# Gathering the tokens of an expert: by rows sorted in memory instead of by a 0/1 matrix product

## What is computed

```python
def moe_swiglu(x, w_router, w_gate, w_up, w_down):
    logits = (x @ w_router).astype(jnp.float32)
    top_val, top_idx = lax.top_k(logits, TOP_K)
    wts = jax.nn.softmax(top_val, axis=-1)
    gates = jnp.sum(jax.nn.one_hot(top_idx, N_EXPERTS, dtype=jnp.float32) * wts[..., None], axis=-2)
    out = jnp.zeros_like(x)
    for e in range(N_EXPERTS):
        h = jax.nn.silu(x @ w_gate[e]) * (x @ w_up[e])
        out = out + gates[..., e:e + 1].astype(x.dtype) * (h @ w_down[e])
    return out
```

## Time and profile before

| | us |
|---|---|
| median of the three runs | 1912.5 |
| the three runs | 1922.28, 1911.4, 1912.5 |
| the profiled execution's own time | 1912.93 |
| its span (first to last instruction) | 1911.2 |

### The profile page before, as it was taken

The page is one execution under the profiler, slowest core; times in us unless marked ns, Lnnn a source line. Parts: engine busy times, 40 slices in busy tenths (PEclk is TensorE's granted clock), DMA queues, the critical chain, the costliest instruction groups (busy, mean ns, idle before and its releaser), DMA issues.

```text
span 1911.2 us, 23856 instructions
## 1 busy us (share of the span) xinstructions
PE 1775.3 (93%) x9639; PEld 1516.7 (79%) x9639; DVE 1448.3 (76%) x1270; ACT 1024.6 (54%) x804; POOL 34.1 (2%) x34
## 2 busy tenths in 40 slices
PE   2899889988979999896999999999999999999995
PEld 2888678968769997896888887888878888888884
DVE  5786865485865554675888889888888898888995
ACT  1434244453223332332776768767777677676772
POOL 0000002000000000000000000000000000000000
PEclk8899989999999999897999999999999999999998
DMA  9578254504734465443999999999999999999992
GB/s 339 195 297 330 102 218 169 183 1 149 201 131 166 144 241 183 170 175 112 334 341 352 364 371 349 342 349 367 361 334 337 368 366 349 352 360 373 354 371 102
DMA packets 214023, 511.32 MB, mean 268 GB/s; under 512 B 6998, under 2 KB 13294, under 8 KB 213913
## 3 DMA queue, kind: packets, MB, share of 16 engines
q1 hardware_dynamic: 209104, 502.46, 72.5%
q10 hardware_dynamic: 4632, 6.72, 1.0%
q0 software_dynamic: 176, 0.53, 0.1%
HBM read 507.77 MB, written 1.93 MB: 267 GB/s over the span
## 4 chain that ended last, share of the span: by engine, by line
PE 88%; DVE 6%; ACT 2%; issue 2%; DMA 1%; POOL 1%; ACTq 0%; POOLq 0%; DVEq 0%
PE psum L719 27%; PE psum L721 27%; PE psum L720 27%; PE psum L1045 2%; PE psum L1073 1%; PE psum L981 1%; DVE units L1474 1%; DMA ring<-in_mod_w 1%; POOL root_out L1441 1%; PE psum L1114 1%; DVE stats L1884 1%; DVE R L1548 0%; DVE x L1893 0%; DMA R<-in_positions 0%; DVE R L1881 0%
## 5 line engine op out<-in xcount | busy, mean ns | idle before, releaser
L1474 DVE TENSOR_TENSOR units<-ring,units 128x2048 fp32r<-128x2048 f32 x451 | 1012.7, 2278 | 239.7 <-ACT units L1180 166.8
L1382 ACT CAST units<-ring 128x2048 fp32r<-128x2048 f32 x332 | 629.7, 1914 | 245.1 <-PE psum L721 147.1
L719 PE MATMUL psum<-units,xr 128*128 128x512 f32 x1120 | 444.7, 397 | 8.0 <-issue 4.5
L721 PE MATMUL psum<-units,xr 128*128 128x512 f32 x1120 | 439.0, 392 | 0.0
L720 PE MATMUL psum<-units,xr 128*128 128x512 f32 x1120 | 438.6, 392 | 0.0
L1180 ACT CAST units<-ring 128x2048 fp32r<-128x2048 f32 (+1 forms) x119 | 218.4, 1879 | 218.3 <-PE psum L721 184.3
L719 PE MATMUL psum<-units,H 128*128 128x512 f32 x696 | 273.4, 393 | 2.2 <-DVE H L1474 2.2
L721 PE MATMUL psum<-units,H 128*128 128x512 f32 x696 | 271.5, 390 | 0.0
L720 PE MATMUL psum<-units,H 128*128 128x512 f32 x696 | 271.4, 390 | 0.0
L719 PE MATMUL psum<-xr,units 128*128 128x256 f32 x864 | 247.2, 286 | 12.4 <-DVE units L1474 11.4
L719 PEld LDWEIGHTS psum<-units,xr 128*128 128x128 f32 x1120 | 212.0, 189 | 52.8 <-issue 7.6
(11 more groups left out here) (243 smaller groups left out, 1092.0 us busy)
## 6 DMA issues: line engine op xcount, KB each, us to landing
ring<-in_moe_w_gate SPq DMA_DIRECT2D x56, 2048.0 KB, 9.4
ring<-in_moe_w_up SPq DMA_DIRECT2D x56, 2048.0 KB, 9.6
ring<-in_moe_w_down SPq DMA_DIRECT2D x56, 2048.0 KB, 9.5
ring<-in_mod_w SPq DMA_DIRECT2D x12, 2048.0 KB, 9.8
ring<-in_ret_w_in SPq DMA_DIRECT2D x11, 2048.0 KB, 10.2
ring<-in_fox_w_in SPq DMA_DIRECT2D x8, 2048.0 KB, 8.9
ring<-in_sc_w_in SPq DMA_DIRECT2D x6, 2048.0 KB, 7.8
ring<-in_ffn_w_gate SPq DMA_DIRECT2D x5, 2048.0 KB, 7.8
```

Source lines behind the costliest of these rows:

```text
L719: mm(dst, left[0], right[0], start=first, stop=False)
L721: return mm(dst, left[1], right[0], start=False, stop=last)
L1382: nc.scalar.copy(*expert_unit_parts(q, j, half, 0)).then_inc(unit_high, 1)
L1474: return v.tensor_tensor(dst, src, high.bitcast(F32), ALU.subtract)
```

## The change

Six things are new.

1. A table `x_rows` of 16 x 128 rows of 1024 numbers in the chip's memory, and an input `zeros` of 128 rows of zeros. During the loads of the dense FFN SP copies `zeros` 16 times into `x_rows`, four copies behind each of four `ffn_up` loads.
2. `places` on DVE, 11 small instructions behind `select(0, 0)`: for each token and each of its two experts the row number, expert times 128 plus place.
3. POOL writes the tokens by these numbers into `x_rows`: four indirect DMAs, of 128 rows of 4 KB each, behind the root `mix1_1` in its list.
4. `load_rows_of` on SP, between the loads j = 3 and j = 4 of each expert but the last: 128 rows (512 KB) of the next expert come back into one of the two tiles of `x`. It waits for the four writes, for the copies of `x` into `e_acc`, and for the gather before.
5. `gather_rows` on PE in the place of `gather` for experts 1 to 7: eight 128x128 transposes of the tile that was loaded. Expert 0 is gathered as before.
6. The wait for `e_sel`, which `gather` had, now stands ahead of its transposition in the down product.

```diff
+    x_rows = nc.dram_tensor("x_rows", (2 * NE, P, D), F32).ap()
...
+        place = sb("place", [P, 2, NT], I32)
...
                     stack(3)
+                for c in range(1, 5):
+                    if at == WEIGHTS_AT[CHUNK_AT["ffn_up", c]]:
+                        for n in range(4 * (c - 1), 4 * c):
+                            sp.dma_start(x_rows[n], t["zeros"]).then_inc(rows_cleared, 16)
+
+            def load_rows_of(e, q):
+
+                sp.wait_ge(rows_placed, 2 * NT * 16)
+                sp.wait_ge(gate_emptied, 2)
+                sp.wait_ge(up_emptied, 2)
+                sp.wait_ge(gather_filled, e)
+                sp.dma_start(x[:, q, :], x_rows[bass.ds(e, 1), :, :].rearrange("o p d -> (o p) d")).then_inc(rows_in, 16)
 
             def expert(e, q, more, number):
                 for j in range(PER_EXPERT):
+                    if j == 4 and more:
+                        load_rows_of(e + 1, 1 - q)
...
-            sweeps(sp, expert)
+            sweeps(sp, expert, lambda: load_rows_of(NE, 0))
...
+            def gather_rows(e, q):
+
+                pe.wait_ge(rows_in, 16 * e)
+                for k in range(KB):
+                    last = nc.tensor.transpose(psum[:, k // 4, (k % 4) * P:(k % 4 + 1) * P], x[:, q, k * P:(k + 1) * P], ident)
+                last.then_inc(gather_filled, 1)
...
                     if j == GATHER_AFTER and more:
-                        gather(e + 1, 1 - q)
+                        gather_rows(e + 1, 1 - q)
...
                         b = turn_bank(PAIRS - 1)
+                        pe.wait_ge(sel_ready, e + 1)
...
             def start_second():
-                gather(NE, 0)
+                pe.wait_ge(scatter_emptied, NE + 1)
+                gather_rows(NE, 0)
                 wide_product(NE, 0, 0)
...
+                if name == "mix1_1":
+                    pool.wait_ge(rows_cleared, 2 * NE * 16)
+                    pool.wait_ge(place_ready, 2)
+                    pool.wait_ge(x_ready, 4 * NT)
+                    for k in range(2):
+                        for tt in range(NT):
+                            at = bass.IndirectOffsetOnAxis(place[:, k, tt:tt + 1], 0)
+                            nc.gpsimd.indirect_dma_start(x_rows.rearrange("e p d -> (e p) d"), at, x[:, tt, :], None
+                                                         ).then_inc(rows_placed, 16)
...
+            def places():
+
+                step(v.tensor_scalar(rt[:, LG], rt[:, C], float(P), float((NE - 1) * P), ALU.is_gt, ALU.mult))
+                step(v.tensor_tensor(rt[:, LG], rt[:, LG], rt[:, C], ALU.add))
+                step(v.scalar_tensor_tensor(rt[:, LG], row8, -float(P), rt[:, LG], ALU.mult, ALU.add))
+                for k, hot in enumerate((OH1, OH2)):
+                    step(v.tensor_tensor(rt[:, LG2], rt[:, LG], rt[:, hot], ALU.mult))
+                    step(v.tensor_reduce(rt[:, 12, :, 0], rt[:, LG2], AX.X, ALU.add))
+                    step(v.tensor_scalar(rt[:, 13, :, 0], rt[:, 12, :, 0], float(NE * P - 1), None, ALU.add))
+                    v.tensor_copy(place[:, k, :], rt[:, 13, :, 0]).then_inc(place_ready, 1)
...
             select(0, 0)
+            places()
             gathered(0, 0)
...
+    given["zeros"] = np.zeros((P, D), np.float32)
```

More of the change, by code:

```diff
@@ L437, in build @@
         out_b = region(13312, D)
+        rows_cleared = sem("rows_cleared")
+        place_ready = sem("place_ready")
+        rows_placed = sem("rows_placed")
+        rows_in = sem("rows_in")
         slot_filled = [sem(f"slot_filled{s}") for s in range(RING)]
```

## The result

| | us |
|---|---|
| before, median of four runs | 1912.4 (1911.4 to 1922.3) |
| the changed kernel, median of four runs | 1897.1 (1896.9 to 1898.0) |
| ratio | 0.9909, 95% interval 0.9881 to 0.9936 |
| the profiled execution's own time, and its span | 1897.09, 1894.9 |

A forecast was written before the change was run, and what follows sets the result against it. PE was taken as the bound, each us off it counting until loads are late. 1912.9 - 18.3 (gathers) + 2.0 (row loads) + 0.5 (start) = 1897.1, said as 1897; the forecast's own range 1893 to 1903, overall 1893 to 1912.

The forecast's parts named there:

- PE's saving: Gathers of seven experts: eight transposes (0.87 us) replace the 3.49 us matrix product, 2.62 us less each, 18.3 in all.
- The loads behind it: 512 KB of rows ahead of load j = 4 in seven experts: 0.3 us lost per expert, 2 us in all.
- PE's cushion: First half of chunk j = 5 ready 1.4 us before PE wants it, against 1.36 us of delay by the row load.
- The hole at j = 4: Around load j = 4 of an expert, 1.7 us of DMA engines stand idle and take most of the row load's 1.36.
- The start: Before expert 0: the four indirect writes end at 900.9 or some 2 us later; 0.5 us lost, once.
- The zeros: Dense FFN: 16 copies of 512 KB, at most 10.8 us per four against some 14 us of slack; cost nothing.
- (a): Rival, experts: the loads become the bound, 1.5 to 2.6 us lost per expert, 1905 to 1913 us; chance 0.11.
- (b): Rival, experts: the load of the rows holds the queue, up to 27 us slower, 1939; chance 0.06 together with (e).
- (c): Rival, start of expert 0: slow writes by index delay load j = 4, up to 17 us once, 1913; chance 0.05.
- (d): Rival, gathers: transposes at 0.088 us and nothing lost, 1893.4 us or a little below; chance 0.06.
- (e): Rival, experts: memory's long-run limit binds; at 352 GB/s 126.7 us per expert, 1937; chance 0.06 together with (b).

The follow-up runs named there:

- The 32 transposes: The changed kernel with each gather by rows doing its eight transposes four times over, all DMAs of the change kept: 1914.4 us, ratio 0.9998.

## Why the prediction was right, and where it was lucky

Forecast 1897, measured 1897.1. The mechanism was right; that the number agrees to the tenth is not, for terms were a little off in both directions and their errors cancel.

- **PE's saving** was taken as 2.62 us per gather, 18.3 in all, from 0.109 us per transpose. It is 2.70 and 18.9. The next product starts sooner behind a transpose than another transpose does: 0.80 us from start to start, inside the bounds of 0.70 to 0.91. The earlier trace rows had it already: four transposes take 0.43 us up to the gather and 0.35 up to a wide product, and 0.87 less these 0.08 is 0.79. The 32 transposes confirm the term: 18.3 us for seven times 24 records.
- **The loads behind it** were given 2.0 us. They cost nothing (the run without them). This price is the step that failed. The room was nearly right: 387 GB/s, read from 5 us stretches, stands beside 389 to 394 over whole experts, and 5.4 us to spare beside 6 to 7. With that room in the same paragraph, I still charged 0.3 us per expert, since I took the long gather for what refills PE's cushion. I would say now that the cushion is refilled in every chunk, wherever the queue runs ahead of PE; that is argued, not shown. In the changed kernel the first half of the same chunk j = 5 is ready at 1044.51 + 2.25 = 1046.8 and wanted at 1055.07 - 5.5 = 1049.6: 2.8 us, where the kernel before had 1.4:

```profile
1044.51 4.49 DVE L1512 TENSOR_TENSOR units<-ring,units 128x2048 fp32r<-128x2048 f32 x2
...
1055.07 0.60 PE L1100 MATMUL psum<-const,R 128*128 128x128 f32 x4
```

- **The hole at j = 4** was real but not needed: ahead of j = 6 the load is as free.
- **The start**, 0.5 us, is 0. The writes were forecast to be over between 900.9 and some 2 us later; SP goes on at 902.15, in a trace that runs 0.7 us behind. An indirect write costs POOL 0.97 us by the median, as the plain DMA of the earlier trace rows had let expect, and load j = 4 is issued at 902.75, before the 905.4 from which it would be noticed. Expert 0's j = 4 to 7 show no idle time. The writes land 3.7 us after their issue (the median in each of the eight later traces; the first one lists no landing), between the 4.4 of the earlier trace rows and the 3.2 that the Trainium skill's formula (DMA: Bandwidth & Descriptors, Anatomy of one DMA) gave; neither value would have moved the sum.
- **The zeros** at nothing: right, with room for twice as many.
- **What I had not in the sum** are the 3.1 us of jumps, clock and the rest. They are as large as the 2.5 us that I had added for stalls that didn't come and the 0.6 by which I had undervalued the saving, together. A forecast from the mechanism alone, taken off the same execution of the kernel before, would have said 1894. That execution, 1912.9, was itself on the low side: the later lots of that kernel have medians of 1914.7 and 1914.1, while the changed kernel again took 1897.3. Counted from 1914.7, the saving of 18.9 and the 0.4 us outside the span give 1896.2, and little is left for chance.

The rivals: (a), the loads as the bound, is false for this change and begins to hold with 3 MB more per expert. (b) fell with the run without the loads, and PE never waited for `rows_in`. (c) fell with the start of the trace. (d), below 1893.4, didn't come, as no stall went. (e), the limit of the memory: the expert of 3 MB more moves 390 GB/s on average for 121 us and that of 5 MB more 393 for 126 us, beyond the 352 that I took as its worst. The Trainium skill's 358 GB/s (DMA: Bandwidth & Descriptors, Bandwidth) as the side that binds between HBM and SBUF doesn't hold here, where one core of the chip works; its remark that single-core figures go higher does.

## What to carry to other kernels

Where PE is the bound and the profile shows room on the DMA engines, work that only moves rows (a product with a 0/1 matrix) can go to the queues, and its worth is then simply the records taken off PE. How much room there is can't be read from the DMA share, which PE's own pace sets (0.97 here, with 8 to 9% to spare): load the queue with useless transfers until PE first waits, and the sum of bytes at that point gives the floor. And when a forecast hits, set the same events of both timelines side by side all the same: here 18.9 us gained and 3.1 us that no term covered stood behind a difference of 15.8.

## What the runs showed of the hardware

- A DMA share of 0.97 to 1.00 looked like a full queue and wasn't: with 3 MB more it rose to 1.03 while the rate went from 364 to 390 GB/s. I read it as time in which packets are under way, which stretches when the engines are less pressed; that is a reading, and no run shows it by itself.
- An f32 transpose of 128x128 is one record, an f32 matmul of the same size two, and each takes 0.11 us from start to start. The numbers of records are what such a gain is counted in: 24 records fewer, 2.70 us.
- A jump of the loop over expert pairs stalls PE for 1.6 to 3.9 us of "issue", behind the first two of the three passes, with the gather by product and by rows. In all ten traces the granted clock is at its lower level, 1.2 GHz, for 3.4 us or more behind at least one of the two, so a jump costs up to 4.8 us in all in the two kernels. That is more than the gather's whole gain in one expert; a loop written out wasn't tried.
- A write by index of 128 rows of 4 KB costs POOL 1 us and lands 3.7 us after its issue, at the start of the experts, where SP holds the next weights back; a read by index in expert 7, beside the weights, cost POOL 1.8 to 2.9 us and landed after 8.1.
